# Another order of passes in the first expert layer, its last pass into the second lane, and the layer norms' sums in banks 0 and 1

## The reference, cut to what matters

```python
x = layer_norm(DN_ALPHA * x + g1 * y, ln1_g[l], ln1_b[l])
h2 = (x * (1.0 + sc2) + sh2).reshape(bsz * n_lat, d)
...
x = layer_norm(DN_ALPHA * x + g2 * ff_lat, ln2_g[l], ln2_b[l])

def moe_ffn(h, w_router, e_bias, w_gate, w_up, w_down, s_gate, s_up, s_down):
    scores = jax.nn.sigmoid((h @ w_router).astype(jnp.float32))
    _, idx = lax.top_k(scores + e_bias.astype(jnp.float32), TOP_K)
    wts = jnp.take_along_axis(scores, idx, axis=-1)
    wts = wts / wts.sum(-1, keepdims=True) * ROUTE_SCALE
    ...
        a = jax.nn.silu(xb @ w_gate[e]) * (xb @ w_up[e])
        return a @ w_down[e]
    ...
    shared = (jax.nn.silu(h @ s_gate) * (h @ s_up)) @ s_down
    return routed + shared
```

## Time and profile before

| | us |
|---|---|
| median of three runs | 3506.56 |
| profiled execution, its own time | 3510.23 |
| its span, first to last instruction | 3508.5 |
| TensorE matmuls busy | 3232.0 (92%) |
| VectorE busy | 1368.3 (39%) |
| ScalarE busy | 522.9 (15%) |
| GpSimd busy | 396.4 (11%) |
| chain that ended last: TensorE | 73% |
| the same: DMA | 13% |
| mean granted clock of TensorE | 0.97 |

### The profile page before, as it was taken

How to read it: one execution, slowest core, us unless ns; L and a number is a source line. 1 busy time by engine, 2 the same in 40 slices (tenths; PEclk the granted TensorE clock), 3 DMA queues, 4 the chain that set the end, 5 groups by cost and what they waited for, 6 DMA issues and landing times.

```text
span 3508.5 us, 39750 instructions
## 1 busy us (share of the span) xinstructions
PE 3232.0 (92%) x14346; PEld 2180.2 (62%) x14346; DVE 1368.3 (39%) x3065; ACT 522.9 (15%) x1094; POOL 396.4 (11%) x452
## 2 busy tenths in 40 slices
PE   7999989999999998999999988999985999989897
PEld 5888868888888887888564433343433576333333
DVE  4766434565025565576463322222213033111112
ACT  2200122001011003100132111111111021101111
POOL 0000021001010000000121211121112101000000
PEclk8999999999999999999999999999997999999999
DMA  7687524774436772576100589999994214999996
GB/s 297 242 328 289 211 96 173 296 286 156 150 118 239 290 269 76 192 258 253 62 13 36 203 301 383 375 371 348 354 364 166 112 37 182 395 411 411 414 407 249
DMA packets 135155, 860.79 MB, mean 245 GB/s; under 512 B 20416, under 2 KB 23872, under 8 KB 37440
## 3 DMA queue, kind: packets, MB, share of 16 engines
q1 hardware_dynamic: 94128, 665.89, 48.3%
q0 software_dynamic: 40128, 191.41, 15.8%
q10 hardware_dynamic: 720, 1.13, 0.1%
HBM read 846.28 MB, written 35.13 MB: 251 GB/s over the span
## 4 chain that ended last, share of the span: by engine, by line
PE 73%; DMA 13%; DVE 7%; issue 4%; ACT 1%; POOL 1%; SPq 0%; POOLq 0%; DVEq 0%; ACTq 0%
PE ps L764 14%; PE ps L1114 13%; DMA ring<-stream_in 10%; PE ps L1393 10%; PE ps L1095 9%; PE ps L861 8%; PE ps L1417 6%; PE ps L1435 2%; PE ps L1354 1%; DVE arena L1932 1%; DMA arena<-mod_stream_in 1%; PE ps L776 1%; PE ps L819 1%; PE ps L828 1%; PE ps L1216 1%
## 5 line engine op out<-in xcount | busy, mean ns | idle before, releaser
L1393 PE MATMUL ps<-ring,arena 128*64 128x512 f32 (+2 forms) x2112 | 578.2, 647 | 112.5 <-DMA ring<-stream_in 103.2
L1393 PEld LDWEIGHTS ps<-ring,arena 128*64 128x64 f32 (+2 forms) x2112 | 206.1, 154 | 431.6 <-issue 425.6
L1932 DVE SCALAR_TENSOR_TENSOR arena<-arena,cond 128x512 f32<-128x512 f32 x602 | 426.7, 749 | 88.6 <-DMA arena<-mod_stream_in 79.4
L1114 PE MATMUL ps<-arena,ring 128*128 128x256 f32 x2048 | 445.1, 379 | 4.5 <-DVE arena L2246 4.5
L1114 PEld LDWEIGHTS ps<-arena,ring 128*128 128x128 f32 x2048 | 387.9, 190 | 57.5 <-issue 5.5
L1095 PE MATMUL ps<-H,ring 128*128 128x256 f32 x1920 | 421.7, 380 | 0.2
L1095 PEld LDWEIGHTS ps<-H,ring 128*128 128x128 f32 x1920 | 363.4, 191 | 50.1 <-issue 1.7
L1417 PE MATMUL ps<-ring,arena 128*64 128x512 f32 (+2 forms) x1056 | 287.9, 609 | 20.4 <-issue 13.6
L1583 ACT ACTIVATE arena<-ps 128x512 f32<-128x512 f32 (+2 forms) x339 | 172.2, 508 | 767.1 <-PE ps L764 318.4
L2453 DVE TENSOR_TENSOR arena<-arena,ps 128x256 f32<-128x256 f32 x76 | 32.0, 422 | 642.1 <-ACT arena L1813 642.1
L1417 PEld LDWEIGHTS ps<-ring,arena 128*64 128x64 f32 (+2 forms) x1056 | 95.5, 146 | 185.1 <-issue 173.0
(11 more groups left out here) (284 smaller groups left out, 3263.3 us busy)
## 6 DMA issues: line engine op xcount, KB each, us to landing
ring<-stream_in SPq DMA_DIRECT2D x612, 1024.0 KB
arena<-mod_stream_in POOLq DMA_DIRECT2D x130, 1024.0 KB, 5.1
arena<-mod_stream_in SPq DMA_DIRECT2D x8, 1024.0 KB, 13.2
YS<-mod_stream_in SPq DMA_DIRECT2D x6, 1024.0 KB, 5.3
arena<-stream_in SPq DMA_DIRECT2D x4, 1024.0 KB, 5.9
moe_out<-zeros POOLq DMA_DIRECT2D x10, 256.0 KB, 4.2
stat<-stream_in SPq DMA_DIRECT2D x2, 1024.0 KB, 5.1
moe_in<-YS POOLq DMA_DIRECT2D x1, 2048.0 KB, 7.6
```

Source lines behind the costliest of these rows:

```text
L1114: m = mm(out[:, i * T:(i + 1) * T], w[:, c * P:(c + 1) * P], f_h[:, 16 * half + c, :], start=(half == c == 0), stop=(half == 1 and c == 15))
L1393: m = mm(out[at, :], e_xt[:, k % 2, 4 * part + c, at], w[:, c * TC:(c + 1) * TC], start=(part == c == 0), stop=(part == 1 and c == 3))
L1932: ins = stt(acc, w, x, acc, MUL, ADD)
```

## The change: what it does

1. `moe_rounds` writes the first layer's 48 passes in another order: S S P P P P, then H O S P four times, S, then SSP seven times, S P S S. H is a solo pass of a heavy rank (0 to 3); the O pass right behind it has that rank's rows past 128 in its first 64 places and a light rank (28 to 31) in the others. The two trios are gone. There are still 28 solo passes, 20 with two ranks, and 192 pieces.
2. The last pass scatters into the second lane, with `lane_loaded` as its signal, and doesn't wait for the scatter before it. The first lane's four loads start when all scatters but the last are in; the second lane is loaded behind them in four blocks once the last scatter is in. Each block has its own signal (semaphores that are free by then, `lane_ready`).
3. The layer norms' sums and squares lie in banks 0 and 1 in place of 6 and 7.
4. `count_spares` and what depends on it moves behind pass 1 on VectorE in both expert layers, and to pass 3 on GpSimd. GpSimd scales the residual one chunk a pass in passes 3 to 10, in place of all eight between the second and third gather.

```diff
-        order["ln", 2 * l] = Phase([6, 7], 0)
+        order["ln", 2 * l] = Phase([0, 1], 0)
...
-        order["ln", 2 * l + 1] = Phase([6, 7], 0)
+        order["ln", 2 * l + 1] = Phase([0, 1], 0)
...
-    def __init__(self, ranks, first=0):
-        self.ranks, self.first = ranks, first
+    def __init__(self, ranks, firsts=None):
+        self.ranks, self.firsts = ranks, firsts or (0,) * len(ranks)
...
-def three_for_two(r):
-    return [Round((r,)), Round((r + 1,)), Round((r, r + 1), P)]
-
-
 def moe_rounds():
-    solo, pair = (lambda r: [Round((r,))]), (lambda r: [Round((r, r + 1))])
-    first = three_for_two(0) + pair(28) + pair(30) + three_for_two(2) + pair(32) + pair(34)
-    quad = lambda r: [Round(tuple(range(r, r + 4)))]
-
-    def in_turn(kinds, at):
+    def in_turn(kinds, at, light=0):
         rounds = []
         for kind in kinds:
-            made, count = {"S": (solo, 1), "P": (pair, 2), "Q": (quad, 4)}[kind]
-            rounds += made(at[kind])
-            at[kind] += count
+            if kind == "O":
+                r = at["H"] - 1
+                rounds.append(Round((r, light + r), (P, 0)))
+            else:
+                count = {"H": 1, "S": 1, "P": 2, "Q": 4}[kind]
+                rounds.append(Round(tuple(range(at[kind], at[kind] + count))))
+                at[kind] += count
         return rounds
 
-    first += in_turn("SP" * 3 + "SSP" * 10 + "PS", {"S": 4, "P": 36})
+    first = in_turn("SSPPPP" + "HOSP" * 4 + "S" + "SSP" * 7 + "SPSS", {"H": 0, "S": 4, "P": 32}, 28)
     second = in_turn("SPQSPPQ" * 4, {"S": 0, "P": 8, "Q": EXPERTS - 32})
     return [Experts(first), Experts(second)]
...
+        mod_loads_of_half = 1 + sum(len(m["jobs"]) * m["turns"] for key, m in MOD_PLAN.items() if key[0] in ("up", "down"))
+        lane_ready = [(ff_set, 16 * 12), (h2_stored, 16 * 4)] + [(full, 16 * (mod_loads_of_half + 1)) for full in mod_full]
...
-                    for r, at in rounds[k].lanes:
+                    for (r, at), first in zip(rounds[k].lanes, rounds[k].firsts):
                         for tb in range(nb):
                             out, places, n = onehot[:, k % 2, tb, at], count1[:, 0:at.stop - at.start], rank[:, tb, r:r + 1]
-                            if rounds[k].first:
-                                last = ts(out, places, n, -float(rounds[k].first), SUB, ALU.is_equal)
+                            if first:
...
+                    elif l == 0 and k == len(rounds) - 1:
+                        ts(slot_out[:, at], token, float(FAR + LANE_B), None, ADD)
...
-                count_spares(l, nb)
-                n_spare = spares(dve, l)
...
-                for b in range(2):
-                    with dve.If(n_spare > b):
-                        spare_pick(b, b)
...
                 for k in range(len(rounds)):
+                    if k == 2:
+                        count_spares(l, nb)
+                        n_spare = spares(dve, l)
+                        for b in range(2):
+                            with dve.If(n_spare > b):
+                                spare_pick(b, b)
                     if l == 0:
                         rows_turned(k + 2)
...
                 for tb in range(nb):
-                    dve.wait_ge(lane_loaded, 16)
                     dve.wait_ge(ff_loaded[tb], 32)
+                    dve.wait_ge(*lane_ready[tb])
                     tt(e_acc[:, tb, :], e_acc[:, tb, :], lane_rows[:, tb, :], ADD).then_inc(sums_ready, 1)
...
-            def scale_residual(n):
+            def scale_residual(n, c):
 
                 cols = TC if n < 2 else T
                 if n < 3:
                     pool.wait_ge(hm_pool, 8 * n + 8)
-                for c in range(DC):
-                    pool.wait_ge(hm_dve, 8 * n + c + 1)
-                    g.tensor_scalar(X[:, c, 0:cols], X[:, c, 0:cols], DN_ALPHA, None, MUL).then_inc(x_alpha, 1)
+                pool.wait_ge(hm_dve, 8 * n + c + 1)
+                g.tensor_scalar(X[:, c, 0:cols], X[:, c, 0:cols], DN_ALPHA, None, MUL).then_inc(x_alpha, 1)
...
-                last_pair = max(k for k, rd in enumerate(rounds) if rd.pair)
+                n_rounds = len(rounds)
+                assert l or not (rounds[-1].pair or rounds[-2].pair)
...
-                scale_residual(2 * l + 1)
                 gather(2)
                 gather(3)
                 if l == 0:
                     pool.wait_ge(ff_set, 16 * (8 + 2))
-                n_spare = spares(pool, l)
...
-                if l:
-                    wait_filled(pool, ph, HIDDEN_T, 0)
-                    first_picks()
-
                 for k in range(len(rounds)):
                     gather(k + 4)
+                    if 3 <= k < 3 + DC:
+                        scale_residual(2 * l + 1, k - 3)
+                    if l and k == 3:
+                        n_spare = spares(pool, l)
+                        first_picks()
                     if l == 0:
                         if k == 2:
                             for i in range(2 * nb):
                                 wait_drained(pool, head, 2 * nb + SHARED + i)
                             pool.dma_start(ff[LANE_B:LANE_B + cols].rearrange("(a p) n -> p a n", p=P), e_acc[:, 0:nb, :]).then_inc(ff_set, 16)
                             pool.wait_ge(ff_set, 16 * (8 + 3))
+                        if k == 3:
+                            n_spare = spares(pool, l)
                             first_picks()
                         for half in range(2):
                             wait_drained(pool, ph, OUTPUT + half, k)
-                        wait_past(pool, scattered, 16 * k)
-                        if k == last_pair + 1:
-                            pool.dma_start(lane_rows[:, 0:nb, :], ff[LANE_B:LANE_B + cols].rearrange("(a p) n -> p a n", p=P))\
-                                .then_inc(lane_loaded, 16)
+                        if k < n_rounds - 1:
+                            wait_past(pool, scattered, 16 * k)
                         at = k % RECORDS
                         pool.sem_inc(rows_moved, 1)
-                        rows = slot_out if rounds[k].pair else slot_token
+                        rows = slot_out if rounds[k].pair or k == n_rounds - 1 else slot_token
                         pool.indirect_dma_start(ff[0:LANE_B + cols], bass.IndirectOffsetOnAxis(rows[:, at:at + 1], 0), e_y[:, k % 2, :], None,
-                                                bounds_check=LANE_B + cols - 1, oob_is_err=False, compute_op=ADD).then_inc(scattered, 16)
+                                                bounds_check=LANE_B + cols - 1, oob_is_err=False, compute_op=ADD)\
+                            .then_inc(scattered if k < n_rounds - 1 else lane_loaded, 16)
                 if l == 0:
-                    pool.wait_ge(scattered, 16 * len(rounds))
+                    pool.wait_ge(scattered, 16 * (n_rounds - 1))
...
                 with pool.If(n_spare > 0):
+                    if l == 0:
+                        pool.wait_ge(lane_loaded, 16)
                     spare_rows(0, 0)
...
                 for tb in range(nb):
                     pool.dma_start(e_acc[:, tb, :], ff[tb * P:(tb + 1) * P]).then_inc(ff_loaded[tb], 16)
+                pool.wait_ge(lane_loaded, 16)
+                for tb in range(nb):
+                    pool.dma_start(lane_rows[:, tb, :], ff[LANE_B + tb * P:LANE_B + (tb + 1) * P]).then_inc(lane_ready[tb][0], 16)
```

More of the change, by code:

```diff
@@ L270, in __init__ @@
         self.last = last
[L271 removed]
+        self.cap = [max(rd.firsts[rd.ranks.index(r)] + P // len(rd.ranks) for rd in rounds if r in rd.ranks) for r in range(EXPERTS)]
         assert sorted(self.order) == [(r, part) for r in range(EXPERTS) for part in range(3)]
[L275 to L276 removed]
 def moe_rounds():
[L280 to L284 removed]
+    def in_turn(kinds, at, light=0):
         rounds = []
         for kind in kinds:
[L287 to L289 removed]
+            if kind == "O":
[5 more added lines that the diff above has]
+                at[kind] += count
         return rounds
[L292 removed]
+    first = in_turn("SSPPPP" + "HOSP" * 4 + "S" + "SSP" * 7 + "SPSS", {"H": 0, "S": 4, "P": 32}, 28)
     second = in_turn("SPQSPPQ" * 4, {"S": 0, "P": 8, "Q": EXPERTS - 32})
@@ L2415, in one_hot @@
                         wait_filled(dve, ph, SLOT, k - 2)
-                    for r, at in rounds[k].lanes:
+                    for (r, at), first in zip(rounds[k].lanes, rounds[k].firsts):
                         for tb in range(nb):
                             out, places, n = onehot[:, k % 2, tb, at], count1[:, 0:at.stop - at.start], rank[:, tb, r:r + 1]
-                            if rounds[k].first:
-                                last = ts(out, places, n, -float(rounds[k].first), SUB, ALU.is_equal)
+                            if first:
+                                last = ts(out, places, n, -float(first), SUB, ALU.is_equal)
                             else:
@@ L2906, in _ @@
                     modulate_context(2 * l)
```

(3 more changed lines are left out.)

3 lines of the change are left out of this document (1 added, 2 removed).

## The result

The changed kernel took 3461.04 us (median of 4 runs, 3456.9 to 3462.09) against 3506.21 of the kernel before on the same chip (3503.05 to 3507.59). The ratio is 0.987, 95% interval 0.9853 to 0.9887: 45.2 us less. The forecast was 3462 us, 44.2 less. The sum holds, but three of its terms don't, and their errors cancel.

A forecast was written before the change was run, and what follows sets the result against it. Transfers were taken to bound the first expert layer, with idle time lost to ring slots held. Layer 32.9 + tail 7 + norm 5 - last norm 0.7 = 44.2 us less, from 3506.56 to 3462 us; range 3445 to 3489.

The forecast's parts named there:

- hole 2: First expert layer, 2057 to 2107 us, loads at 254 GB/s: the new order closes it, 15.4 us less.
- The end: End of the first expert layer: the last stall frees one piece later, 3 us given back.
- hole 1: First expert layer, 1958 to 2031 us: slots come back earlier, 8 more pieces landed, 26.2 us less.
- This is not a term of its own.: Pass 0's gate-up starting 8.7 us earlier without the count only moves slot releases, so it adds nothing separately.
- The count's cover in pass 2: VectorE's 10 us count in pass 2 is hidden by the pair pass being loaded: cost 0, up to 10.
- Tail: End of the first expert layer: the last scatter, in the other lane, is issued earlier, 7 us less.
- Norm: Norm behind the first expert layer: with bank 0 the sums start when the transposes end, 5 us less.
- Last norm: Last layer norm: its sums start two halves later because bank 0 comes fifth, 0.7 us more.
- C: Rival: the order of passes gives nothing, only tail and norm gain 11.3 us, 3495 us; chance 0.10.
- B: Rival: slots stay short around H and O passes, hole 2's time returns in four small ones, 3478 us; chance 0.16.
- E: Rival: slower, each of the four H passes blocks the ring as the old trios did, 3524 us; chance 0.04.
- D: Rival: all that the three windows lack is made up, 59 us less 8.7 given back, 3445 us; chance 0.08.

The follow-up runs named there:

- e2: The kernel before with only the layer norms' sums moved to banks 0 and 1: 3499.65 us, ratio 0.9983.
- e3: The kernel before with only VectorE's count moved to pass 2 and GpSimd's residual scaling cut into eight parts: 3499.70 us, ratio 0.9985.
- e10: The changed kernel with VectorE's count back ahead of the first rows, the scaling still in eight parts: 3461.01 us, ratio 0.9869.
- e1: The kernel before with only the new order of passes: 3484.65 us, ratio 0.9939.
- e5: The changed kernel with its start kept and two trios in place of the four H and O pairs: 3481.62 us, ratio 0.9929.
- e7: The changed kernel without the first lane's four loads, whose rows are missing from the sums: 3453.28 us, ratio 0.9849.
- e12: The changed kernel with all eight end loads issued behind the last scatter, a block of each lane in turn: 3459.89 us, ratio 0.987.
- e6: The changed kernel with the old tail: one 2 MB second-lane load, last scatter waiting for the one before: 3463.51 us, ratio 0.9877.
- e4: The changed kernel with the old trios back at the start and the last passes pair, solo, solo: 3488.23 us, ratio 0.9951.

## Why the prediction was right, and where it was not

**Holes.** The mechanism was right: ring slots held over a trio starve the loads. By 2031 us 9.86 MB more had been loaded. These are 9.4 pieces, 30.8 us at the 3.28 each of the forecast, where I had 8 pieces or 26.2 less 5.7 for the lane's write. By 2107 us it was 14.34 MB, so hole 2 gave 4.48 MB or 12.2 us, against 15.4. The end gave back 0.5 and not 3: the layer's last load was issued 46.0 us earlier and the last expert matmul ended 45.5 earlier. Together 42.5 us; the layer's own length fell by 44.0 in the first pair of traces and by 38 to 40 against e2's. I had 32.9, and the term that was mis-sized is the piece count of hole 1. I also priced hole 1 at the loads' own rate (3.28 us a piece, 0.32 MB per us) and hole 2 at that of all queues (0.367), which leaves the sum loose by some 15%.

**"This is not a term of its own."** This is the step that failed. I took the earlier start of pass 0 as included in the count of slots. e3 has it alone and gains 3.5 MB, 9 to 13 us of layer, and 5 to 7 us of time; in the loads' bytes it adds to the order in full. Its start is 5.8 us earlier and its gate-up 2.7 shorter, 8.5 together, where I had 8.7: TensorE gives the slots back and the loads idle until then, so the shift came through to the loads. With it the order's own 10.7 pieces (11.21 MB) become 13.7; I had 11 for both. And I didn't see what made the start late: I laid the whole delay on VectorE's count, priced the cut scaling at 0, and looked for its cost in passes 3 to 10. e10 shows that moving the scaling alone gives 4.9 of the 5.7 us. The earlier trace rows lay at the same microseconds; I didn't ask whether the one lengthened the other.

**The count's cover in pass 2** held: it ran from 2006.58 us and VectorE's next rows came at 2012.85, TensorE without a gap there.

**Tail**, 7 us: measured 2.2 in the profile. The shift of the issue came (2609.52 is 1.62 behind the last expert matmul, forecast 1.7), and the scatter was 0.7 shorter. What failed is "the second lane's four loads follow its landing as the first lane's did before": their median is 10.1 us and not 5.3, behind 2 MB of the first lane. From the last scatter's landing to the first transposes passed 11.1 us (2620.38 to 2631.52) where it had been 6.1: 6.5 and 0.7 gained, 5.0 lost. I had named the sharing for the scatter and not for the loads behind it. I also missed that the order moves the 2 MB load ahead of another scatter and among the ring's loads, which is why parts measured alone don't tell the tail's share.

**Norm**, 5 us: 7.7 from the first transposes to the sums' end in the first pair, 7.1 between before and e2 (20.67 against 13.55), a little beyond my far bound of 6.9. The sums ran at full clock, which that bound assumed, and the transposes ahead of them took 5.6 us where they had taken 6.6. **Last norm**: +0.78, as forecast (0.7).

**Rivals.** C falls with e1, B and E with the windows and e5. D, all that the three windows lacked made up, didn't come: from 1958 to 2001 us the engines moved 205 GB/s and not 367. The layer fell by 38 to 44 us; I had 32.9, and D needs 50.3 (59 less 8.7), so it came out about midway.

**The signs.** The DMA share (0.86 from 1975 to 2031 us), the early gate-up and the sums right behind the transposes came as forecast. The last expert matmul ended at 2607.90 us and not near 2620, and the transposes started 23.6 us behind it and not 18 to 19: the same two errors, of layer and tail.

**The sum.** By the traces 38 to 44 for the layer, 9.2 to 9.9 for tail and norm, less 0.8: 46 to 53; by the medians 45 to 47. I forecast 44.2 by an underrated layer and norm and an overrated tail. That the total came within 1 us of the measured median was luck.

## What to carry to other kernels

With a ring of slots, count how many passes the oldest slot is held and what may be loaded meanwhile; a pass that needs old and new pieces together costs an idle queue, and it is worth most to avoid it while the ring first fills. When an instruction is removed from in front of a waiting engine, look at what else ran at the same microseconds: a neighbour on another engine may have lengthened it, and moving either may be enough. And where one transfer is moved on a queue, look at the one that now stands behind it.

## What the runs showed of the hardware

- Some of VectorE's small operations took 2 to 4.6 times as long while GpSimd ran over 128x512 tiles: 0.17 to 0.79 us for a copy of 128x2, 0.74 to 1.56 for three 128x64 operations. Others didn't change: eight TENSOR_SCALAR of 128x1 took 1.46 us in before and in e10.
- A scatter that adds 128 rows at the end of the layer landed in 9.3 to 11.8 us, with or without the first lane's loads beside it (11.53 in e7 and 11.19 in e12 without them, 10.86 in after with them). It took 19.8 and 20.0 us right behind a 2 MB load on the same queue while the ring's loads kept the DMA engines busy 0.94 to 0.97 of the time (e6, e1), 11.6 and 11.8 behind the same load once they had let up (before, e3), and 6.0 to 6.1 when little else ran (45 GB/s in e6 from 2630 to 2635 us).
- 512 KB loads from GpSimd's queue took 5.3 to 5.6 us (median) as four alone. As eight they took 9.5 and 10.1 with the first four beside a scatter (after), and 6.9 and 7.6 issued behind it over 4.8 us (e12).
- The core's DMA engines moved 366 to 369 GB/s over the 473 us from 2107 us in every kernel but e5 (359, with a trio there), and from 2031 to 2057 us 394 to 407 in those that begin with S S P P P P, 381 to 394 in before, e2, e3 and e4.
- TensorE's granted clock stood at 0.50 from 2660 to 2680 us before, after TensorE had been idle from 2653.41 us on.
